# Experts of 96 places: token columns in groups of 64 and 32, weights streamed past them

## The reference

```python
def moe_ffn(h, w_router, w_gate_up, w_down):          # h: (1, 256, 1024)
    t = h.reshape(B * S, D)
    logits = (t @ w_router).astype(jnp.float32)       # 8 experts
    top_val, top_idx = lax.top_k(logits, TOP_K)       # 2 of 8
    top_w = jax.nn.softmax(top_val, axis=-1)
    combine = jnp.sum(jax.nn.one_hot(top_idx, N_EXPERTS) * top_w[..., None], axis=1)
    out = jnp.zeros((B * S, D), jnp.float32)
    for e in range(N_EXPERTS):
        gt, up = jnp.split(t @ w_gate_up[e], 2, axis=-1)      # 1024 x 2816
        y_e = (jax.nn.silu(gt) * up) @ w_down[e]              # 1408 x 1024
        out = out + combine[:, e:e + 1] * y_e
    return out
```

## Time and profile before

| | |
|---|---|
| time, median of 3 runs (lowest to highest) | 2596.46 us (2596.38 to 2596.57) |
| profiled execution, its time | 2596.57 us |
| its span in the profile | 2594.8 us |
| mean granted TensorE clock | 0.968 |
| TensorE busy | 2432.6 us, 94% of the span |
| VectorE busy | 978.5 us, 38% |
| ScalarE busy | 404.7 us, 16% |
| moved by DMA | 426.90 MB, mean 165 GB/s |

### The profile page before, as it was taken

One profiled execution on the slowest core, in us unless ns is written; L12 is line 12 of the kernel. 1 busy time (PEld: TensorE's weight loads), 2 busy tenths in 40 slices (PEclk: granted clock), 3 DMA queues, 4 the chain that ended last, 5 costly groups with the idle time before them and its releaser, 6 DMA issues.

```text
span 2594.8 us, 32157 instructions
## 1 busy us (share of the span) xinstructions
PE 2432.6 (94%) x13320; PEld 1720.5 (66%) x13320; DVE 978.5 (38%) x1890; ACT 404.7 (16%) x905; POOL 71.1 (3%) x91
## 2 busy tenths in 40 slices
PE   6999999899999987999998999999978899999998
PEld 4444444344444464678885578887747799999997
DVE  3585562545442028745415744513344200000002
ACT  2211340100000021510001221003222200000001
POOL 0210210000000000000000000000020000000000
PEclk9999999999999998999999999999988899999999
DMA  8433421245335221058852148865322288888883
GB/s 305 151 131 130 148 80 65 97 147 176 129 121 132 87 106 33 34 194 296 271 171 101 55 140 284 298 169 187 127 86 66 90 262 266 267 268 268 266 260 116
DMA packets 377315, 426.90 MB, mean 165 GB/s; under 512 B 11539, under 2 KB 293682, under 8 KB 376938
## 3 DMA queue, kind: packets, MB, share of 16 engines
q1 hardware_dynamic: 373136, 419.79, 49.5%
q10 hardware_dynamic: 4058, 5.35, 0.7%
HBM read 423.88 MB, written 1.13 MB: 164 GB/s over the span
## 4 chain that ended last, share of the span: by engine, by line
PE 87%; DVE 8%; ACT 1%; DMA 1%; issue 1%; ACTq 0%; POOL 0%; SPq 0%; DVEq 0%; POOLq 0%
PE banks L496 77%; DVE mem L1348 2%; DVE mem L1345 1%; PE banks L1230 1%; ACT mem L2155 1%; PE banks L1244 1%; PE banks L727 1%; DVE mem L1341 1%; PE banks L1079 1%; DVE mem L1696 1%; PE banks L762 1%; PE banks L505 1%; DVE mem L1750 1%; DVE mem L1393 1%; PE banks L565 1%
## 5 line engine op out<-in xcount | busy, mean ns | idle before, releaser
L496 PE MATMUL banks<-mem 128*128 128x256 f32 (+5 forms) x9776 | 2069.1, 383 | 56.2 <-ACT mem L2155 32.6
L496 PEld LDWEIGHTS banks<-mem 128*128 128x128 f32 (+3 forms) x9776 | 1465.8, 183 | 654.4 <-issue 504.1
L1345 DVE SCALAR_TENSOR_TENSOR mem<-mem 128x512 f32<-128x512 f32 (+5 forms) x596 | 383.3, 677 | 21.7 <-ACT mem L2155 9.9
L1348 DVE TENSOR_TENSOR mem<-mem,banks 128x256 f32<-128x256 f32 (+2 forms) x108 | 58.1, 538 | 825.9 <-ACT mem L2155 796.9
L2155 ACT ACTIVATE mem<-banks 128x512 f32<-128x512 f32 (+4 forms) x262 | 118.7, 470 | 1233.1 <-PE banks L496 1090.8
L2155 ACT ACTIVATE mem<-mem 128x256 f32<-128x256 f32 (+7 forms) x431 | 186.0, 484 | 758.4 <-DVE mem L1345 531.6
L1345 DVE SCALAR_TENSOR_TENSOR mem<-banks,mem 128x256 f32<-128x256 f32 (+7 forms) x258 | 133.8, 544 | 434.5 <-PE banks L496 345.5
L1348 DVE TENSOR_TENSOR mem<-mem 128x256 f32<-128x256 f32 (+12 forms) x221 | 79.1, 366 | 36.5 <-ACT mem L2155 23.7
L505 PE MATMUL banks<-mem 128*128 128x128 f32 (+2 forms) x320 | 51.6, 310 | 38.4 <-DMA mem<-in_gdn_conv_w 12.4
L505 PEld LDWEIGHTS banks<-mem 128*128 128x128 f32 (+2 forms) x320 | 41.5, 162 | 55.2 <-DVE mem L1341 20.6
L1348 DVE TENSOR_TENSOR mem<-banks,mem 128x256 f32<-128x256 f32 (+4 forms) x104 | 43.2, 417 | 76.8 <-PE banks L496 45.8
(11 more groups left out here) (168 smaller groups left out, 737.1 us busy)
## 6 DMA issues: line engine op xcount, KB each, us to landing
mem<-in_ada_w SPq DMA_DIRECT2D x96, 1024.0 KB, 9.9
mem<-in_moe_w_gate_up SPq DMA_DIRECT2D x80, 1024.0 KB, 9.2
mem<-in_ffn_w_in SPq DMA_DIRECT2D x44, 1024.0 KB, 7.0
mem<-in_moe_w_down SPq DMA_DIRECT2D x32, 768.0 KB, 4.7
mem<-in_ffn_w_out SPq DMA_DIRECT2D x32, 704.0 KB, 6.8
mem<-in_ffn_w_gate_up SPq DMA_DIRECT2D x22, 1024.0 KB, 6.6
mem<-in_moe_w_down SPq DMA_DIRECT2D x32, 640.0 KB, 5.9
mem<-in_ab_w_in SPq DMA_DIRECT2D x16, 1024.0 KB, 7.0
```

What stands on the lines that cost most here:

```text
L496: ins = nc.tensor.matmul(o, lhsT, rhs, start=start, stop=stop)
L1345: return V.scalar_tensor_tensor(out=o, in0=a, scalar=sc, in1=b, op0=op0, op1=op1)
L1348: return V.tensor_tensor(o, a, b, op)
```

## The change

The sparse branch has 96 places per expert (`CAP`) instead of 128, and is taken when `most` is at most 96. The places are used as 64 and 32.

- Gate and up now have the tokens as the stationary operand and the weights streaming, as down had. The 64 first places are loaded into two column groups of the array (64 columns each), which each take 256 of a panel's 512 weight columns (`first_half`); the 32 others into four column groups, which each take 128 (`rest`). Results have places on partitions.
- A panel is 512 columns wide (384 in the third): gate and up are separate panels, used together as a pair, three pairs instead of six panels. Down has two pairs instead of four panels: features 0 to 767 and 768 to 1407 of 512 columns. The number of panels per expert stays ten and that of transfers twenty; the pieces of a row are 2048 bytes (1536 in the third pair) instead of 1024.
- `panel(..., beside=True)` marks the second of a pair. `held` counts the panels that are to be released; the first matmul of the next pair releases both.
- VectorE multiplies silu(gate) by up into `e_tok`, places on partitions. `turn_acts` turns these by three transposes per pair, and ScalarE copies them to `e_own` (`acts_turned`), two or three copies per pair. For the first two pairs this stands between `first_half` and `rest` of the next pair, for the third behind the gather.
- The gather of the next expert moves behind the third pair, its places are 96 columns. The scaled pick matrices are made twice, for the 64 and the 32 places (`pick_half`, `pick_rest`), repeated along the columns so that their transposes hold them on each row group; four transposes (`turn_picks`) instead of two.
- Down works in the same two forms, 64 and 32 columns of activations. `put_back` multiplies row groups: 8 matmuls on 64 rows and 8 on 32.
- The dense branch takes the same new panels. The router's first matmul now releases the panel before it.

The diff, cut to its core:

```diff
+CAP = 96
...
+                        for q in range(3):
+                            w = T2 if q < 2 else 3 * P
+                            for first in (0, FE):
+                                load(8, w, [(slice(k, k + 4), slice(0, w),
+                                             gu[:, bass.ds(e * KD + k, 4), first + q * T2:first + q * T2 + w]) for k in (0, 4)])
...
-                    ins.then_inc(s["panel_used"], 1)
-                    fresh[0] = False
+                    ins.then_inc(s["panel_used"], fresh[0])
+                    fresh[0] = 0
...
-                fresh[0] = not (m.i is None and m.n == 1)
+                if beside:
+                    held[0] += 1
+                else:
+                    fresh[0], held[0] = held[0], 1
...
+                def first_half(e, q, wg, wu):
+                    c["gu"].next()
+                    pe.wait_ge(s["gu_taken"], c["gu"].ahead(0))
+                    bank = PS[c["gu"].place(2)]
+                    for i, w in enumerate((wg, wu)):
+                        for k in range(8):
+                            for g in range(2):
+                                n = L if q < 2 or g == 0 else P
+                                last = mm(bank[g * HD:(g + 1) * HD, i * L:i * L + n], h_own[:, e % 2, k, 0:HD], w[:, k, g * L:g * L + n],
+                                          k == 0, k == 7)
+                def rest(e, q, wg, wu):
+                    for i, w in enumerate((wg, wu)):
+                        for k in range(8):
+                            for g in range(4 if q < 2 else 3):
+                                last = mm(bank[g * 32:g * 32 + 32, i * P:(i + 1) * P], h_own[:, e % 2, k, HD:CAP],
+                                          w[:, k, g * P:(g + 1) * P], k == 0, k == 7)
+                def turn_acts(q, n):
+                    pe.wait_ge(s["gu_taken"], 2 + n)
+                    bank, tok = moved_item(), e_tok[:, n // 2 % 2 ^ 1, :]
+                    turn(bank[:, 0:P], tok[:, 0:P])
...
-                with pe.If(most <= P):
+                with pe.If(most <= CAP):
...
+                        for q in range(3):
+                            width = T2 if q < 2 else 3 * P
+                            wg, wu = panel(8, width), panel(8, width, beside=True)
+                            if q == 0:
+                                pe.wait_ge(s["moved_taken"], gathered)
+                            first_half(e, q, wg, wu)
+                            if q:
+                                turn_acts(q - 1, c["gu"].n - 1)
+                            rest(e, q, wg, wu)
                             if q == 0 and e:
                                 put_back(e - 1, done)
...
+                        if e < NE - 1:
+                            gathered = gather()
+                        turn_acts(2, c["gu"].n)
+                        if e < NE - 1:
+                            turn_picks()
+                        for m in range(2):
+                            w1, w2 = panel(6, T2), panel(5, T2, beside=True)
                             bank = moved_item()
+                            if m == 0:
+                                pe.wait_ge(s["moved_taken"], c["moved"].n - (2 if e < NE - 1 else 1))
+                            for k in range(KE):
+                                for g in range(2):
+                                    last = mm(bank[g * HD:(g + 1) * HD, 0:L], e_own[:, k, 0:HD], of(k)[:, g * L:(g + 1) * L], k == 0, k == KE - 1)
+                            for k in range(KE):
+                                for g in range(4):
+                                    last = mm(bank[g * 32:g * 32 + 32, L:3 * P], e_own[:, k, HD:CAP], of(k)[:, g * P:(g + 1) * P],
+                                              k == 0, k == KE - 1)
```

More of the change, by code:

```diff
@@ L351, in build @@
         h_tok = work(7168, 2, D)
[L352 to L355, removed]
+        h_own = work(9216, 2, KD, CAP)
+        pick = work(10752, 2, CAP)
+        pick_half = work(10944, 2, 2 * HD)
+        pick_rest = work(11200, 2, P)
+        back = work(11456, 2, 2, L)
+        y_own = work(12480, 2, 3 * P)
         slots = work(13312, NE + 2, 2)
@@ L1191, in _ @@
                 await_h(1)
+                fresh[0], held[0] = held[0], 0
                 for t in range(2):
@@ new lines, in rest @@
+                def rest(e, q, wg, wu):
+                    c["gu"].next()
+                    pe.wait_ge(s["gu_taken"], c["gu"].ahead(0))
+                    bank = PS[c["gu"].place(2)]
+                    for i, w in enumerate((wg, wu)):
[3 more added lines that the diff above has]
+                                          w[:, k, g * P:(g + 1) * P], k == 0, k == 7)
+                    last.then_inc(s["gu_ready"], 1)
@@ L1247, in _ @@
+                    for m in range(2):
+                        for i in range(4):
+                            r = slice(i * 32, (i + 1) * 32)
+                            last = nc.tensor.matmul(moe_sum(4 * m + i), y_own[r, m, L:3 * P], back[r, e % 2, 1, :],
+                                                    start=False, stop=e == NE - 1, skip_group_check=True)
+                    last.then_inc(s["out_ready"], 8)
                 pe.wait_ge(s["tok_copied"], 4)
-                with pe.If(most <= P):
+                with pe.If(most <= CAP):
@@ L1290, in _ @@
                                 nb = 2 if q < 5 else 1
-                                w = panel(8, 2 * nb * P)
+                                if q % 2 == 0:
+                                    width = T2 if q < 4 else 3 * P
+                                    both = panel(8, width), panel(8, width, beside=True)
                                 c["gu"].next()
@@ L2551, in _, with silu @@
+                def silu(width):
+                    await_("gu_ready", "gu")
+                    act.wait_ge(s["gu_taken"], c["gu"].ahead(0))
+                    pl = c["gu"].place(2)
+                    ac(e_silu[:, pl, 0:width], PS[pl][:, 0:width], ACT.Silu).then_inc(s["silu_ready"], 1)
+                with act.If(most <= CAP):
                     gathered(0)
+                    moved(back[:, 0, :, :].rearrange("p a n -> p (a n)"), T2)
                     for e in range(NE):
-                        for q in range(6):
-                            nb = 2 if q < 5 else 1
-                            await_("gu_ready", "gu")
-                            act.wait_ge(s["gu_taken"], c["gu"].ahead(0))
-                            pl = c["gu"].place(2)
-                            ac(e_silu[:, pl, 0:nb * P], PS[pl][:, 0:nb * P], ACT.Silu).then_inc(s["silu_ready"], 1)
-                            if q == 2 and e < NE - 1:
-                                gathered(1 - e % 2)
@@ L2563, in _ @@
+                        for m in range(2):
+                            moved(y_own[:, m, :], 3 * P)
                 for n, x in c.items():
```

142 lines of the change are left out of this document (80 added, 62 removed).

## The result

The changed kernel took 2652.32 us, the median of four runs (2650.18 to 2655.35), beside 2596.52 (2596.38 to 2597.5) for the kernel before on the same chip: a ratio of 1.0215, 95% interval 1.0197 to 1.0233. It is slower, as forecast, but by 56 us and not by 25.5, and above the range.

What follows compares the result with a forecast made beforehand. TensorE bounds the kernel before; paired loads would turn its gain into waits. Six cycles +25.2 us, first expert +2.4, last -0.8, small terms -0.05; +25.5 was taken, from 2596.57 to 2622 us, eight-in-ten range 2597 to 2643.

Steps and rivals of the forecast that it cites:

- TensorE's work: Expert stage: TensorE's steps at full clock sum to 57.0 us per expert, against 66.5 before.
- The ring: Four panel slots: each step lasts its matmuls or the next pair's load, whichever is longer; 68.7 us per expert.
- The clock: Expert stage: the 6 us wait ahead of q0 lowers TensorE's clock, costing 1.8 us.
- q0: An expert's first gate/up pair with the put-back: 14.2 us at full clock, 16.0 with the clock lost.
- q2: An expert's third gate/up pair with the next expert's gather: 16.6 us, longer than the 11.1 us load beside it.
- The transfer: Weight loads from first issue to landing: 13.4 us for 4.19 MB, 11.2 for the third pair, 10.1 for a down pair.
- q1: An expert's second gate/up pair: 11.2 us of matmuls, set to 12.2 by the load of q2.
- the cycle: Time from put-back to put-back, one expert: 70.7 us forecast, 4.2 more than 66.5.
- The ends: Outside the six cycles: first expert +2.4 us, last expert -0.8, shorter put-back at the end -0.2.
- More is slow on TensorE: Rival, expert stage: 64-column form at 127 ns and clock down in q2 too; 74.8 us a cycle, 2655 us; chance 0.10.
- The quicker transfers: Rival, weight loads: transfers land sooner, 2587 us with the clock kept or 2591 with it lost; chance 0.17.
- the held clock: Rival, expert stage: clock holds in the waits, loads as forecast; 68.7 us a cycle, 2608 us; chance 0.11.

Runs made afterwards that it cites:

- e1: Changed kernel, but each panel is waited for and released by itself instead of in pairs; 2528.69 us, ratio 0.9744.
- e2: Changed kernel, but panels are released one by one while TensorE still waits for both of a pair; 2585.76 us, ratio 0.9964.
- e6: Changed kernel with gate and up panels alone waited for and released one by one, down still in pairs; 2543.02 us, ratio 0.9801.
- e10: Changed kernel with down panels alone waited for and released one by one, gate and up still in pairs; 2598.81 us, ratio 1.0012.
- e9: Changed kernel with the 32-token matmuls replaced by few long ones, output incomplete; 2620.85 us, ratio 1.0089.
- e7: e1 with the last put-back done bank by bank, so VectorE's adds may start after the first bank; 2540.48 us, ratio 0.9789.
- e3: Changed kernel with constant matmuls in TensorE's waits ahead of the second down pair and q0; 2637.15 us, ratio 1.0165.
- e4: Changed kernel with only one of eight steps of the 32-column gate and up matmuls, output incomplete; one run, 2615.18 us.

## Why the prediction was right in sign and wrong in size

By its own steps:

- **TensorE's work, 57.0 us an expert: right.** Pairs 7.1 + 3.7, the turn 0.55 (0.4 was taken), gather 3.8, put-back 3.15 (3.4), down 7.5. e1 shows the sum.
- **The ring: right.** Each step is as long as its matmuls or the next pair's load. e1 removes the pairs and with them all of the loss; e2, e6 and e10 take parts.
- **The clock: right in kind, a little short.** It restarts at 0.50 to 0.56 at every q0; q0's 64- and 32-column matmuls take 13.3 us on the mean instead of 10.85, so 2.5 us and not 1.8, and q0 16.4 instead of 16.0. In one of six experts the wait ahead of q2 was 4.2 us and cost the clock as well (8.78 us for 7.1).
- **The transfer: the step that failed.** 13.4, 11.2 and 10.1 us were forecast, 14.5, 12.2 and 11.3 came. The fixed part and the rate were read rightly: a load of e9 without a fetch packet takes 13.3 and 10.2. What the sum left out is that every load of this kernel meets a fetch of the program, which holds one of the 16 DMA engines for 1.1 us, and a load is whole only when its slowest engine is. The three steps that a load bounds are longer by it: q1 (13.2 for 12.2), the first down step (12.4 for 11.1) and the second (15.9 for 14.8), 3.4 of the 3.8 us by which the cycle of 74.5 exceeds the 70.7 forecast. e9 shows the cause for the loads that TensorE waits for in the down steps. In q1 the trace shows a second way. The third pair's load lands in 10.7 to 10.9 us in e10, although a fetch packet falls into it there too, some 9 us on. In after the second of its four issues is held up on SyncE. The second issue in after, then in e10:

```profile
2210.13 1.33 SPq L379 DMA_DIRECT2D mem<-in_moe_w_gate_up  x1
```

```profile
2125.87 0.37 SPq L379 DMA_DIRECT2D mem<-in_moe_w_gate_up  x1
```

In all six experts of after this issue took 0.88 to 1.60 us, 0.9 more than 0.37 on the mean, and each time it ended 0.4 us behind the end of a fetch packet that was under way (here 2211.07). Of all second issues of after's expert stage the nine with such a packet took 0.65 us or more, the 29 others 0.37. That fits q1's 1.0 and was read from the traces; no run changed the issue alone.

- **The ends.** The first expert came to 67.1 us (+4.0 for +2.4), by the same loads. The last gained nothing (+0.2 for -0.8). Behind the last put-back's start 24.5 us are left and not 22.7: +1.8 where -0.2 was forecast. VectorE's eight adds now begin 3.2 us after it, since the one increment hangs on the last of the put-back's matmuls:

```profile
2624.42 2.00 PE L1294 MATMUL banks<-mem 64*128 64x256 f32 x16 [0.61 <-ACT mem L2228]
...
2627.63 3.23 DVE L1415 SCALAR_TENSOR_TENSOR mem<-banks,mem 128x256 f32<-128x256 f32 x8 [26.60 <-PE banks L1299]
```

I had looked at the put-back's length and not at what the moved increment holds back. e7, which was to show it, ran into another cost; so this point is read from the trace, not shown by a run.

Together: 6 x 8.0 + 4.0 + 0.2 + 1.8, less 0.1 ahead of the stage, is +54 in the profiled run (2596.57 to 2650.71); forecast were 25.5.

Of the rivals none happened. "More is slow on TensorE" has a time (2655) near the measured one, by causes that the trace denies: the 64-column form takes 110 ns, not 127, and q2 stays at the full clock in five of six experts. A chance on it would have been right for no reason. The quicker transfers are excluded by 14.5 and 11.2 us, the held clock by the windows. The Trainium skill's formula (DMA: Bandwidth & Descriptors, "Anatomy of one DMA") is fitted on GpSimd's path; an estimate by it for 4.19 MB in one transfer is 11.6 us. Four transfers issued by SyncE took 13.3 even without a fetch packet. The same page of the Trainium skill ("Queues, rings and completion order") has each DMA engine take turns between the queues that have work for it, packet by packet; that fits a weight load that is held up on one engine by another queue's packet.

## What to carry to other kernels

If panels are used in groups, wait for and release each on its own: with a ring of four, pairs cost 16.6 of 74.5 us an expert here, and the same matmuls taken panel by panel made a kernel 2.6% faster than the one before instead of 2.2% slower. When a step is bounded by the landing of one load from idle queues, price the load by its slowest engine, with one packet of the program's fetch in it where many small instructions are run (here one for every 250 to 256 instructions of TensorE). When one increment replaces several, ask who could have started at the first.

## What the runs showed of the hardware that I had not expected

- A fetch of the program (16 KB, some 1.1 us on one DMA engine) can delay the last landing of a weight load by about its own length: 14.5 us for 13.3 at 4.19 MB, 11.3 for 10.2 at 2.88 MB. The count goes with TensorE's instructions: 42 packets in six experts, 20 with about half the instructions; 1000 idle GpSimd instructions an expert added none.
- A fetch packet that is under way when SyncE begins the second issue of a load holds up that issue until 0.4 us behind the packet's end: 0.65 to 1.60 us instead of 0.37, in nine of nine cases in after. The first issue of a load was not held (0.37 us in five of five cases there); third issues were, in e9 and e4 (0.67 to 1.31 us).
- The same 32 matmul instructions of the put-back take 3.15 us at full clock in one order, and in the other 0.265 us each while the clock is full, which would be 8.5 us (an estimate).
- TensorE's clock fell behind 2.7 us of idle (e3) as well as behind 6.1, stayed up once in e3 behind 2.4 us, and was up again some 6 us after the restart (0.50 in 2192.5 to 2197.5, 1.00 from 2199).
